# Long convolution of a hybrid model block: the imaginary products of the spectra on GpSimd, the folds of the second half of the frequencies inside them

## What is computed

```python
def fft_long_conv(z, kern, skip):
    L = z.shape[1]                                     # 512
    zf = jnp.fft.rfft(z.astype(jnp.float32), n=2 * L, axis=1)
    kf = jnp.fft.rfft(kern, n=2 * L, axis=0)
    y = jnp.fft.irfft(zf * kf[None], n=2 * L, axis=1)[:, :L]
    return (y + z * skip).astype(z.dtype)

def hyena_operator(u, short_taps, kern, skip):
    v, x1, x2 = split_cols(centred_conv3(u, short_taps), (HY_WIDTH, HY_WIDTH, HY_WIDTH))
    z = v
    for o, gate in enumerate((x1, x2)):
        z = gate * fft_long_conv(z, kern[:, o], skip[o])
    return z
```

## Time and profile before

| what | us |
|---|---|
| median of 3 runs | 3145.71 |
| lowest and highest | 3133.18, 3148.56 |
| the profiled execution, its own time | 3144.39 |
| its span, first to last instruction | 3142.5 |
| `hy_order0`, first transpose to the first of `hy_order1` | 42.4 |
| `hy_order1`, first transpose to VectorE's last instruction | 44.1 |

### The profile page before, as it was taken

One profiled execution on the slowest core, in us unless ns is written; L12 is line 12 of the kernel. 1 busy time (PEld: TensorE's weight loads), 2 busy tenths in 40 slices (PEclk: granted clock), 3 DMA queues, 4 the chain that ended last, 5 costly groups with the idle time before them and its releaser, 6 DMA issues. The chain is left out here.

```text
span 3142.5 us, 52314 instructions
## 1 busy us (share of the span) xinstructions
PE 2814.3 (90%) x22466; PEld 2165.0 (69%) x22466; DVE 1539.7 (49%) x2519; ACT 1071.8 (34%) x1956; POOL 128.9 (4%) x110
## 2 busy tenths in 40 slices
PE   6799888999988888879999988898887988899997
PEld 2488766777767776358887876566566766788876
DVE  6623247345546666674554243554535436445422
ACT  6411267332224543223222233554224132422222
POOL 0000000000012452000000000000000000000000
PEclk9899999999989998989999989999888999999999
DMA  9411200134100002102332223212111122233321
GB/s 316 133 54 54 51 1 1 54 106 148 45 1 4 4 4 89 68 27 76 99 100 85 94 61 127 80 51 75 48 61 38 51 89 63 67 89 96 98 84 64
DMA packets 221640, 224.31 MB, mean 71 GB/s; under 512 B 27360, under 2 KB 192736, under 8 KB 221345
## 3 DMA queue, kind: packets, MB, share of 16 engines
q1 hardware_dynamic: 221106, 219.78, 23.0%
q10 hardware_dynamic: 304, 1.18, 0.1%
HBM read 207.61 MB, written 12.80 MB: 70 GB/s over the span
## 5 line engine op out<-in xcount | busy, mean ns | idle before, releaser
L212 DVE TENSOR_TENSOR second_w_low<-second_w_raw,second_w_high 128x1024 fp32r<-128x1024 f32 (+1 forms) x236 | 282.2, 1198 | 487.4 <-ACT second_w_high L208 486.6
L208 ACT CAST second_w_high<-second_w_raw 128x1024 fp32r<-128x1024 f32 (+1 forms) x236 | 241.5, 1025 | 683.5 <-PE ffn_in_acc L233 246.6
L231 PE MATMUL ffn_in_acc<-ffn_h_high,second_w_high 128*128 128x512 f32 x704 | 279.5, 397 | 5.2 <-DVE ffn_h_low L670 4.6
L232 PE MATMUL ffn_in_acc<-ffn_h_low,second_w_high 128*128 128x512 f32 x704 | 277.1, 394 | 0.0
L233 PE MATMUL ffn_in_acc<-ffn_h_high,second_w_low 128*128 128x512 f32 x704 | 277.0, 393 | 0.0
L212 DVE TENSOR_TENSOR first_w_low<-first_w_raw,first_w_high 128x1024 fp32r<-128x1024 f32 x91 | 110.5, 1221 | 244.0 <-ACT first_w_high L208 243.9
L208 ACT CAST first_w_high<-first_w_raw 128x1024 fp32r<-128x1024 f32 x91 | 94.4, 1045 | 188.6 <-PE attn_in_acc L233 80.5
L231 PEld LDWEIGHTS ffn_in_acc<-ffn_h_high,second_w_high 128*128 128x128 f32 x704 | 133.2, 189 | 36.7 <-issue 7.4
L231 PE MATMUL attn_in_acc<-attn_h_high,first_w_high 128*128 128x256 f32 (+1 forms) x416 | 143.9, 346 | 15.2 <-DVE attn_h_low L406 15.2
L232 PEld LDWEIGHTS ffn_in_acc<-ffn_h_low,second_w_high 128*128 128x128 f32 x704 | 133.3, 189 | 29.8 <-issue 0.7
L233 PEld LDWEIGHTS ffn_in_acc<-ffn_h_high,second_w_low 128*128 128x128 f32 x704 | 133.2, 189 | 29.5
(11 more groups left out here) (829 smaller groups left out, 6257.0 us busy)
## 6 DMA issues: line engine op xcount, KB each, us to landing
second_w_raw<-in_ffn_w_gate SPq DMA_DIRECT2D x44, 512.0 KB, 3.8
second_w_raw<-in_ffn_w_up SPq DMA_DIRECT2D x44, 512.0 KB, 3.8
second_w_raw<-in_ffn_w_down SPq DMA_DIRECT2D x40, 512.0 KB, 3.5
first_w_raw<-in_rec_w_in SPq DMA_DIRECT2D x33, 512.0 KB, 4.0
second_w_raw<-in_w_in SPq DMA_DIRECT2D x24, 512.0 KB, 3.9
second_w_raw<-in_w_branch_gate SPq DMA_DIRECT2D x24, 512.0 KB, 4.1
first_w_raw<-in_attn_w_in SPq DMA_DIRECT2D x22, 512.0 KB, 3.8
first_w_raw<-in_attn_ada_w SPq DMA_DIRECT2D x12, 512.0 KB, 7.6
```

Source lines behind the costliest of these rows:

```text
L208: act.copy(self.view(self.high[b % self.splits], b), self.view(self.raw[self.ring[b]], b)).then_inc(self.high_done, 1)
L212: dve.tensor_tensor(self.view(self.low[b % self.splits], b), self.view(self.raw[self.ring[b]], b), self.view(self.high[b % self.splits], b ...
L231: pe.matmul(out, sh, mh, start=(first and j == 0), stop=False)
L232: pe.matmul(out, sh, ml, start=False, stop=False)
```

## The change

Each order gets a GpSimd program: when both folds of half w are done, it makes the two imaginary products, L3509 and L3510 of before, into an imaginary tile of its own for each half, and counts up a new semaphore, `imag_crossed`. VectorE's program is cut into three functions called in the order: folds of w = 0, real part of w = 0, folds of w = 1, mix of w = 0, real part of w = 1, mix of w = 1. The real part of w = 1 waits for `mixed`, since the real tile is shared; the mix waits for `imag_crossed`.

```diff
-        real, imag = (st.sb(n, [P, 2, 2, 512]) for n in ("real", "imag"))
+        real, imag = st.sb("real", [P, 2, 2, 512]), [st.sb(f"imag{w}", [P, 2, 2, 512]) for w in range(2)]
...
+        @block.gpsimd
+        def _(pool):
+            for w in range(2):
+                pool.wait_ge(folded, 2 * w + 2)
+                pool.tensor_tensor(imag[w][:, 0], zw[w][:, 0], spectrum[:, 1, :, w], ALU.mult)
+                pool.tensor_tensor(imag[w][:, 1], zw[w][:, 1], spectrum[:, 0, :, w], ALU.mult).then_inc(imag_crossed, 1)
+
...
-            for w in range(2):
+            def folded_half(w):
                 for j in range(2):
                     n = 2 * w + j
                     dve.wait_ge(copied, n + 1)
                     dve.wait_ge(odds, n + 1)
                     fold(dve, zw[w][:, j, 0], zw[w][:, j, 1], even[n % 2][:], ps[2 * (n % 2) + 1][:], j).then_inc(folded, 1)
-                h_real, h_imag = spectrum[:, 0, :, w], spectrum[:, 1, :, w]
+
+            def real_part(w):
                 dve.wait_ge(folded, 2 * w + 2)
-                dve.tensor_tensor(real[:, 0], zw[w][:, 0], h_real, ALU.mult)
-                dve.tensor_tensor(real[:, 1], zw[w][:, 1], h_imag, ALU.mult).then_inc(crossed, 1)
-                dve.tensor_tensor(imag[:, 0], zw[w][:, 0], h_imag, ALU.mult)
-                dve.tensor_tensor(imag[:, 1], zw[w][:, 1], h_real, ALU.mult).then_inc(crossed, 1)
-                dve.wait_ge(crossed, 4 * w // 2 + 1)
+                if w:
+                    dve.wait_ge(mixed, w)
+                dve.tensor_tensor(real[:, 0], zw[w][:, 0], spectrum[:, 0, :, w], ALU.mult)
+                dve.tensor_tensor(real[:, 1], zw[w][:, 1], spectrum[:, 1, :, w], ALU.mult).then_inc(crossed, 1)
+                dve.wait_ge(crossed, w + 1)
                 dve.tensor_tensor(real[:, 0], real[:, 0], real[:, 1], ALU.subtract).then_inc(joined, 1)
-                dve.wait_ge(crossed, 4 * w // 2 + 2)
-                dve.tensor_tensor(imag[:, 0], imag[:, 0], imag[:, 1], ALU.add).then_inc(joined, 1)
+
+            def mix(w):
+                dve.wait_ge(imag_crossed, w + 1)
+                dve.tensor_tensor(imag[w][:, 0], imag[w][:, 0], imag[w][:, 1], ALU.add).then_inc(joined, 1)
...
+            folded_half(0)
+            real_part(0)
+            folded_half(1)
+            mix(0)
+            real_part(1)
+            mix(1)
```

More of the change, by code:

```diff
@@ L3440, in hyena_order @@
         zw = [st.sb(f"spectrum{w}", [P, 2, 2, 512]) for w in range(2)]
-        real, imag = (st.sb(n, [P, 2, 2, 512]) for n in ("real", "imag"))
+        real, imag = st.sb("real", [P, 2, 2, 512]), [st.sb(f"imag{w}", [P, 2, 2, 512]) for w in range(2)]
         ps = [st.ps(f"dft{i}", [P, BANK]) for i in range(4)]
         back = [st.ps(f"idft{i}", [P, BANK]) for i in range(4)]
-        turned, tokens_a, tokens_v, evens, odds, copied, folded, crossed, joined, mixed, backed, scaled, own = (
+        turned, tokens_a, tokens_v, evens, odds, copied, folded, crossed, imag_crossed, joined, mixed, backed, scaled, own = (
             st.sem(x) for x in ("turned", "tokens_a", "tokens_v", "evens", "odds", "copied", "folded", "crossed",
-                                "joined", "mixed", "backed", "scaled", "own"))
+                                "imag_crossed", "joined", "mixed", "backed", "scaled", "own"))
         block = st.block()
@@ L3518, in _ @@
                 dve.wait_ge(joined, 2 * w + 2)
-                dve.tensor_tensor(zw[w][:, 0, 1], imag[:, 0, 0], imag[:, 0, 1], ALU.subtract)
-                dve.tensor_tensor(zw[w][:, 1, 1], imag[:, 0, 0], imag[:, 0, 1], ALU.add).then_inc(mixed, 1)
+                dve.tensor_tensor(zw[w][:, 0, 1], imag[w][:, 0, 0], imag[w][:, 0, 1], ALU.subtract)
+                dve.tensor_tensor(zw[w][:, 1, 1], imag[w][:, 0, 0], imag[w][:, 0, 1], ALU.add).then_inc(mixed, 1)
+            folded_half(0)
[4 more added lines that the diff above has]
+            mix(1)
             for i in range(4):
```

## The result

| what | before | change |
|---|---|---|
| median of 6 runs each | 3139.02 | 3156.44 |
| lowest and highest | 3133.18, 3148.56 | 3152.63, 3159.18 |
| ratio, with its interval | 1 | 1.0053 (1.0039 to 1.0067) |
| the profiled execution, its own time | 3144.39 | 3159.14 |
| its span | 3142.5 | 3157.1 |

The forecast, made for the profiled execution, was 3159; that execution took 3159.14, and the median lies 2.6 us under the forecast. Between the profiled executions the change costs 14.75 us. By the ratio it costs 0.53% (16.6 us), just past the line of 0.5%: the line in the prediction stood at 3161.4 because the first three runs of before had a median 6.7 us above that of six.

What follows compares the result with a forecast made beforehand. VectorE was taken to bound each order from the second fold to the second pass. Two orders at +7.0 us (14.0) plus 0.5 for the clears, over the profiled 3144.39, gave 3159 us; range 3147 to 3166.

Steps and rivals of the forecast that it cites:

- the line in the prediction: Whole kernel: 3161.4 us, 0.5% over a median of 3145.71, beyond which a run would count as slower.
- VectorE's own order costs 0.24: VectorE up to `mixed` = 1: two products fewer, four folds more and a later difference together add 0.24 us.
- GpSimd's product takes 2.34 us: GpSimd's 128x1024 imaginary product, undisturbed: 2.34 us, extrapolated from shorter ones since no row showed that shape.
- Strict turns, four of 2.15, ahead of `mixed` = 1: GpSimd and VectorE alternate on SBUF-only operands; four 2.15 us turns delay VectorE's chain 8.6 us per order.
- the rival of engines side by side: In both orders, GpSimd and VectorE don't hold each other up: 0.7 to 1.8 us gained per order, 3141 to 3144; chance 0.07.
- TensorE starts the first pass at 1343.86, 12.8 behind the transform: TensorE's transform back of w = 0 starts 8.85 us later than before, after a 12.8 us pause.
- The second pass waits for the first, not for VectorE: TensorE's transform back of w = 1: VectorE is ready at 1350.8, but TensorE is free only at 1353.8.
- The first pass takes 9.9 us: TensorE's transform back of w = 0 takes 9.9 us, with 5.6 us at low clock; +7.0 us per order.
- The third rival: TensorE's clock stays low for the whole transform back of w = 0: 3164, or 3168 all at 1.2 GHz; chance 0.17.
- Three clears of 1.2 less 1.9 and 1.2: +0.5: The new semaphore makes clears stand at three places instead of two; TensorE idles meanwhile, adding 0.5 us.
- The bound that I set, +2.6: Upper bound on the cost of the moved semaphore clears, taking 1.9 us for each of the three.
- The chances: Whole kernel against the 0.5% line: slower 0.30, the same 0.69, faster 0.01.

Runs made afterwards that it cites:

- Alone the order: Changed kernel with both imaginary products back on VectorE, GpSimd idle, semaphores cleared at their places of before: 1.0001 of before.
- beside the folds: Changed kernel with GpSimd making only w = 0's imaginary products, started after VectorE's difference, w = 1's on VectorE, semaphore clears placed as before: 1.0011 of before.
- The one product a half: Changed kernel with one imaginary product of each half on GpSimd, the other on VectorE, semaphore clears placed as before: 3132.77 us, one execution.
- the memset: Changed kernel with GpSimd's products replaced by zeroing the imaginary tiles, imaginary products left out, semaphore clears placed as before: 3135.32 us, one execution.
- old clears: Changed kernel with the semaphore count lowered by one per order, so clears stand at nsa_in and dn_scan: 1.0022 of before, a second time 1.0033.
- the change again: The changed kernel as it is, run a second time on another occasion: 1.0061 of before, median 3156.51 us.
- new clears: Kernel before with only the semaphore count raised by one per order, so clears stand at ffn1_down, mem_v and ffn2_in: 1.0019 of before.
- VectorE's products earlier: Kernel before, without GpSimd, the first component's real and imaginary products moved directly behind the first fold of each half: 1.0003 of before.

## Why the prediction was right, and where it was not

*VectorE's own order costs 0.24.* Right: from the start of the transform `mixed` = 1 came 8.70 us later than before, and the turns below are 8.47 of it. Alone the order left `hy_order0` at 42.5.

*GpSimd's product takes 2.34 us.* Right: 2.35 and 2.34 beside the folds. The estimate from the Trainium skill's "GPSIMD Engine Reference" (section "Elementwise — side-by-side cycle accounting") was 2.25; the trace is 4% above it. (The page's figure is for an addition of 2048 columns, where the prediction says a product.)

*Strict turns, four of 2.15, ahead of `mixed` = 1.* Right in number, place and size: 8.47 for 8.6, on the four instructions that were named. The one product a half (one long row of each kind), the memset and the folds (none) leave little else. By the Trainium skill's "SBUF — State Buffer" (section "SBUF: two separate sides") VectorE waits out the whole instruction, and the turn would be 2.42. That estimate is too high: the traces agree with the page on who is held (instructions with both inputs in SBUF, not those with one in PSUM), and measured 2.03 to 2.15. One reading on the way was wrong: the rival of engines side by side was given "most of GpSimd's products in the scan show near their shortest time". The shortest of the twelve of L2763 took 0.727 us and their median is 0.962; in the trace eleven of them took 0.96. So most of these were lengthened, which speaks against that rival.

*TensorE starts the first pass at 1343.86, 12.8 behind the transform.* It did at 1344.11, 12.63 behind it; the stage had begun 0.4 us later.

*The second pass waits for the first, not for VectorE.* Right: VectorE was done 2 us before the second pass started.

*The first pass takes 9.9 us.* Too long: 9.16 and 8.78. The low clock lasted 4.6 us, not the 5.6 that I took from the earlier trace rows. So an order costs 6.1 and 5.8 for 7.0: 11.9 for 14.0. The runs of the change and with old clears gave 11.2 to 13.1 for both orders. The third rival, low clock through the pass, falls: the pause was as long as the one of 12.66 with 10.4 us at 0.50, and the clock was back in less than half of that.

*Three clears of 1.2 less 1.9 and 1.2: +0.5.* This is the term that failed. Its barriers are right: `mem_v` +1.3, `dn_scan` -1.2 where TensorE's busy time stayed the same, and in the change again +2.8 and -2.8, of which 1.6 each is TensorE's busy time. But the step counted the clear as idle time alone. It stands at the start of a stage, where TensorE is already waiting, and so it also changes how long TensorE runs at 1.2 GHz afterwards, in either direction: -3.7 us of busy time in `nsa_in`, where the clear went, +4.1 in `ffn2_in`, where one came. With that the clears cost about 4 us by stages and 6 to 10 by times, against +0.5. The bound that I set, +2.6, was made from barriers too, and was too low by all of these. *Clears 3 to 10 us, forecast 0.5; orders 7 to 13, forecast 14.0*: the sum came out right since the two errors go against each other, which is luck, and the rest of the program was 2.6 us shorter in the profiled execution.

*The chances.* 0.69 stood on a change within 0.5%; the ratio's interval (1.0039 to 1.0067) lies on both sides of that line, and its middle just beyond. The step that failed is where the line was put: 0.5% over a median of 3145.71 is 3161.4, over 3139.02 it is 3154.7, which is less than the forecast itself. Three runs that span 15 us don't place a median well enough for a line 2.5 us from the forecast.

What stays open: `ffn2_down` took 138.4 with the change, twice, but 137.4 and 135.8 with the old clears and 136.0 with the new clears in the kernel before, so its +2.4 isn't tied to the clears. The long stage `rwkv`, ahead of both orders and the same code, took from 309 to 316 us in the profiled executions; one execution each doesn't tell why. And why the same stage's low clock lasts 15 us once and a few another time is not explained by the length of the pause alone: 12.63 us of pause brought 4.6 here.

## What to carry to other kernels

Before work goes from VectorE to GpSimd, look at what VectorE does meanwhile: here, where it read two operands from SBUF, each GpSimd product took nearly its own length out of VectorE's chain (2.15 us for 1.14 saved), and only products beside folds, which have an input in PSUM, and memsets, which read nothing, held nothing up. Follow a delay to the engine that really ends the stage, and ask what its clock does behind the new pause. And a resource that is counted, such as a semaphore, can move things far away: compare the whole program stage by stage, not only the stage that was edited.

## What the runs showed of the hardware that was not expected

- A pause of 1.2 to 1.5 us more at a stage's start (TensorE 5.83 to 6.13 for 4.61), by a clear of semaphores, made the stage 5.0 to 7.0 us longer (`ffn2_in` 261.6 to 261.9 in nine executions, 266.9 to 268.6 in three), as 29 matmuls in the first 6 us at a mean clock of 0.74 became 47 in 15 us at 0.50 in one of the three.
- The low clock isn't lost by shortening one pause: with VectorE's products earlier the first pass ran at 1.00 (7.17 us) and the second took 8.86, where before it was the other way round.
- Where VectorE and GpSimd both have instructions ready, neither keeps the turn: the VectorE rows L3518 and L3520, beside the products of w = 0, and L3526 and L3527, beside those of w = 1, were each held by exactly one GpSimd product, eight times in two orders, and GpSimd's were lengthened to 3.25 to 3.39 except the last of w = 1, 2.78, behind a VectorE instruction of half the width.
- A GpSimd memset of 128x1024 took 0.95 us and held VectorE not at all.
